# Odd head norms from PSUM, MLP squares behind the second ReLU, and masks made earlier in the solve

## The chip, the cores and the metric

The kernel runs on one core of a Trainium2 chip. The metric is the time of the program on the device in microseconds (us), as the median of several runs. The engines are TensorE (PE), VectorE (DVE), ScalarE (ACT) and GpSimd (POOL); SyncE (SP) only issues transfers. They run side by side and are ordered by semaphores.

## The reference, cut to what matters

A token matrix `x` of 256 x 1024 passes through a first block (two kinds of attention, and a retrieval feed-forward over 16384 experts) and a second block of two layers. The change touches the second block alone:

```
layer 0: proj = rms(h) @ w_in_e              # uv | qkv | z | beta | a
         a_out = gmlp(gelu(uv));  b_out = gated_delta_rule(...)   # triangular solves in chunks of 64
         h = h + concat(a_out, b_out) @ w_out_e
layer 1: q, k, v = split(rms(h) @ w_qkv_o)
         q = rms_heads(q, q_gain) * 64**-0.5;  k = rms_heads(k, k_gain)   # 16 pieces of 64 a row
         h = h + diff_attention(q, k, v) @ w_out_o
both:    h = h + square(relu(rms(h) @ w_mlp1)) @ w_mlp2          # 1024 -> 4096 -> 1024
         h = h + (p @ w_ple) * sigmoid(rms(h) @ w_gate)
```

## The kernel before

All matrices stay in SBUF as 128 partitions by two halves of the tokens (`t` = 0, 1: "block 0" and "block 1" of a result). The weights are streamed in 128x1024 chunks through a ring of four slots. SyncE loads `w_raw`; ScalarE rounds it to `w_hi` ("split", L1218); GpSimd makes the rest `w_lo` = `w_raw` - `w_hi` ("rest", L1705). TensorE then does three products for each pair of operands (high with high, high with low, low with high; L611 to L613 where the tokens are stationary, L647 to L649 where the weights are). The splits run three chunks ahead of TensorE. A slot is loaded again when both its `w_hi` and `w_lo` are made. Every engine has its program written out by hand; within an engine all is done in that order, and a wait holds up all that stands behind it. ScalarE's `split_to(j)` makes all splits below chunk j; GpSimd walks through the chunks j and does other things at marked places (`norm_at`, `FIRST[...] + 3`).

**The solve.** `SOLVE` is a list of 21 steps, numbered from 0, each with two halves of four 128x128 products (L1055) in a rotation of six PSUM banks. Results named in `PLAIN` are copied out by ScalarE (L1560), the others are added, subtracted or multiplied by VectorE (L2432 to L2449). Steps 6 and 7 are N4 and N4T (plain), 8 and 9 additions to YI and YIT, 10 is N8 (plain), 11 and 12 additions to YI and YIT, 13 is P1 (plain, from L1T and Y), 14 and 15 subtract from Y and YT, 16 is P2 (from L2T). L1T and L2T are `aT` times a mask. gmlp's mix (L1032) is put before step 11 on TensorE, and its product into OC (L2409) before step 12 on VectorE; TensorE transposes OC before step 15.

**The odd layer.** Groups q1, k1 and v1 have eight chunks each and leave four PSUM banks `acc`; the next group's first product into a bank waits until the bank is read. VectorE copies the banks with the row's factor (L1953), squares (L2557), sums (L2558), waits for ScalarE's root (L1631) and scales by the root and by the gain (L2563, L2564). TensorE transposes Q and K after v1.

**The MLP.** In each layer 64 chunks alternate: one of w_mlp1 whose result (`col`) is 128 hidden units for all tokens, and one of w_mlp2 that adds into `acc`. ScalarE takes ReLU and square (L1584, L1586), VectorE cuts the square into `H_hi` (L2503) and `H_lo` (L2505), and TensorE needs `H_lo` for the chunk of w_mlp2. Three chunks stand ahead of a loop of 15 rounds, one behind it. The row norm of the MLP isn't applied to its input but to its sum: ScalarE squares X (`row_squares`, L1234), GpSimd makes `rstd` (L1759 to L1761) and its square `rsq` (L1844), and VectorE uses `rsq` in the residual (L1964).

Of the kernel before, what the change touches and what calls it, by code (L numbers as in the profile page):

```python
# [33 lines left out]
ACT = mybir.ActivationFunctionType  # L34
# [3 lines left out]
P = 128  # L38
# [149 lines left out]
def share(semaphore, signals):  # L188


    base, shared = 0, {}
    for name, count in signals:
        shared[name] = (semaphore, base)
        base += count
    return shared
# [5 lines left out]
        "qk", "vc", "qup", "kvup", "br_a", "br_b", "wout", "v", "out_e", "mlp0", "ple0", "q1", "k1",  # L201
        "v1", "out_o", "mlp1", "ple1")]),
    **share("acc_read_act", [("ev_ga", 4), ("ev_gb", 4), ("ev_zba", 2), ("ev_uv", 4), ("ev_gate0", 4),
                             ("ev_gate1", 4)]),
# [28 lines left out]
def program(nc, ins, out):  # L233
    ctx = ExitStack()
    with ctx:
# [173 lines left out]
        L1T = big("L1T", 105, [P, NT, G_H, P])  # L409
        P1 = big("P1", 109, [P, NT, G_H, P])  # L410
        L2T = big("L2T", 113, [P, NT, G_H, P])
# [69 lines left out]
        ba = stat[:, 0:16].rearrange("p (t n) -> p t n", t=NT)  # L481
        sp_x, sp_d, sp_r = stat[:, 40:48], sq32[:, 0:8], sq32[:, 16:24]
# [718 lines left out]
        def _(act):  # L1201
# [371 lines left out]

            def mlp(layer):

                j0 = FIRST[f"mlp{layer}"]
                f0 = layer * D_FF // P

                def relu2(blk, j, i, s):
                    used(act, j, i)  # L1580
                    if layer or not (isinstance(blk, int) and blk < 2):

                        act.wait_ge(sem("H"), blk - 1 + f0)
                    f(H_r[:, s, :], col[s][:, 0:SEQ], ACT.Relu).then_inc(sem("relu"), 1)  # L1584
                    act.wait_ge(sem("relu"), blk + 1 + f0)
                    f(H_q[:, s, :], H_r[:, s, :], ACT.Square).then_inc(sem("square"), 1)  # L1586

                split_to(j0 + 4)
                relu2(0, j0, 0, 0)
                split_to(j0 + 5)  # L1590
                relu2(1, j0 + 1, 0, 1)
                split_to(j0 + MLP_SKIP + AHEAD)
                j = j0 + MLP_SKIP
                with act.Fori(0, MLP_ROUNDS) as r:
                    for q in range(4):
                        split(j + q + AHEAD, r)
                        if q % 2 == 0:
                            relu2(2 * r + 2 + q // 2, j + q, r, (q // 2) % 2)
                done[0] = j + 4 * MLP_ROUNDS + AHEAD
# [9 lines left out]
            def per_layer_in(layer):  # L1609

                nc.scalar.dma_start(p_raw[:, :, :], ins["p"][layer]).then_inc(sem("p_in"), 16)

# [3 lines left out]
            row_squares("ev_out_e", (1,))  # L1616
            per_layer_in(0)
# [6 lines left out]
            row_squares("x_ple0", (1,))  # L1624
            for m, nxt in enumerate(("k1", "v1")):
                split_to(FIRST[nxt] + 7)
                if m == 0:
                    act.wait_ge(sem("lam_dots"), upto("lam_dots", 2))
                    f(stat[:, 2:4], stat[:, 0:2], ACT.Exp).then_inc(sem("lam_exp"), 1)
                act.wait_ge(sem("qk_ss"), m + 1)  # L1630
                f(sq32[:, :], sq32[:, :], ACT.Sqrt, bias=epsc[:, 0:1], scale=1.0 / C_DH).then_inc(  # L1631
                    sem("qk_root"), 1)
# [31 lines left out]
            row_squares("ev_out_o", (1,))  # L1664
            per_layer_in(1)
# [6 lines left out]
        def _(pool):  # L1672
# [121 lines left out]
            def delta_and_gmlp_maps():  # L1794
# [14 lines left out]
                for t in range(NT):  # L1809
                    for m in range(M_G):  # L1810
# [14 lines left out]
            norm_at = [FIRST[name] + 3 for name in ("qk", "query", "zba", "mlp0", "ple0", "q1", "mlp1",  # L1825
                                                    "ple1")]
            j = 1
            while j < len(PLAN):
# [11 lines left out]
                for layer in range(2):  # L1840
                    if j == FIRST[f"mlp{layer}"] + 3:

                        have_rstd(pool, R_MLP[layer])
                        g.tensor_tensor(rsq, rstd[:, :], rstd[:, :], ALU.mult).then_inc(  # L1844
                            sem("rsq"), 1)
# [39 lines left out]
        def _(dve):  # L1885
# [515 lines left out]
            for s, (result, _, _, _) in enumerate(SOLVE):  # L2401
                if s == MIX_AT + 1:
# [24 lines left out]
                for t in range(NT):  # L2427
# [11 lines left out]
                    else:  # L2439
                        y = YIT if result.startswith("YT") else YI  # L2440
                        if s in (11, 12):

                            then(v.tensor_tensor(four(L1T if s == 11 else L2T, t), four(aT, t),
                                                 over(masks[:, 4 if s == 11 else 5, :], [P, 4, P], 1),
                                                 ALU.mult))
# [107 lines left out]
            for m, (g, src, gain) in enumerate((("q1", Q1, R_QG), ("k1", K1, R_KG))):  # L2553
                evac(g, half(src), R_ODD)
                x = src[:, :, :].rearrange("p t (n d) -> p (t n) d", d=C_DH)
                y = SQ[:, :, :].rearrange("p t (n d) -> p (t n) d", d=C_DH)
                then(v.tensor_tensor(y, x, x, ALU.mult))  # L2557
                then(v.tensor_reduce(sq32[:, :], y, AX_X, ALU.add), "qk_ss")  # L2558
                dve.wait_ge(sem("qk_root"), upto("qk_root", m + 1))
                then(v.reciprocal(sq32[:, :], sq32[:, :]))  # L2560
                if m == 0:
                    then(v.tensor_scalar(sq32[:, :], sq32[:, :], C_DH ** -0.5, None, ALU.mult))
                then(v.tensor_tensor(x, x, over(sq32[:, :], [P, 32, C_DH], 2), ALU.mult))  # L2563
                then(v.tensor_tensor(x, x, over(rows[:, gain:gain + C_DH], [P, 32, C_DH], 1),  # L2564
                                     ALU.mult), "qk1")
# [130 lines left out]
```

## Time and the profile before

| what | us |
|---|---|
| median of 3 runs | 1833.08 |
| lowest and highest run | 1833.07, 1841.83 |
| the profiled execution's own time | 1837.99 |
| its span, first to last instruction | 1836.3 |
| its mean granted TensorE clock | 0.98 |

All rows shown below are of the one profiled execution, with times from the start of its span. The profiled execution is 4.9 us above the median. The odd layer, the two MLPs and the solve lie behind 1140 us of the span.

### The profile page before, as it was taken

How to read it: one execution, taken by the hardware profiler on the slowest of the kernel's cores; microseconds unless marked ns; L12 is line 12 of the kernel's file. 1: busy time of each engine (PE TensorE's matmuls, PEld its weight loads, DVE VectorE, ACT ScalarE, POOL GpSimd, SP SyncE). 2: the span in 40 equal slices, each digit the busy share in tenths (PEclk: the TensorE clock that was granted, in tenths of full speed). 3: DMA queues.
4: the chain of work that ended last, by engine and by line, in shares of the span. 5: the costliest groups of instructions: out<-in, count | busy, mean ns of one | idle time of the engine just before them, and what ended most of it. 6: DMA issues, size and time to landing. Idle time of an engine off the chain costs nothing.

```text
span 1836.3 us, 32192 instructions
## 1 busy us (share of the span) xinstructions
PE 1746.2 (95%) x10852; PEld 1563.1 (85%) x10852; DVE 941.9 (51%) x1874; ACT 922.2 (50%) x1592; POOL 1051.6 (57%) x542
## 2 busy tenths in 40 slices
PE   8989899999999999999999999889999898799998
PEld 6767799999999998888888787878999776689996
DVE  6563229991777775555555657533111377431113
ACT  5555456666333334444555557325445644455454
POOL 7835578888666664000000087337888696478885
PEclk9999899999999999999999999999999998899999
DMA  6623365555444445555555554015555453145553
GB/s 199 178 81 115 115 218 163 182 182 185 148 138 140 142 144 173 194 193 192 191 192 193 195 172 134 23 60 163 185 184 189 153 163 124 47 156 191 185 188 109
DMA packets 81027, 288.23 MB, mean 157 GB/s; under 512 B 9264, under 2 KB 9264, under 8 KB 80432
## 3 DMA queue, kind: packets, MB, share of 16 engines
q1 hardware_dynamic: 80512, 286.10, 48.0%
q8 instruction: 50, 0.82, 0.2%
q10 hardware_dynamic: 432, 1.05, 0.1%
q14 instruction: 33, 0.27, 0.0%
HBM read 285.01 MB, written 2.10 MB: 156 GB/s over the span
## 4 chain that ended last, share of the span: by engine, by line
PE 86%; DVE 6%; ACT 4%; POOL 2%; issue 2%; DMA 0%; DVEq 0%; ACTq 0%; POOLq 0%
PE acc L611 14%; PE acc L612 14%; PE acc L613 14%; PE col L647 11%; PE col L648 11%; PE col L649 11%; PE mb L904 3%; POOL w_lo L1705 2%; PE acc L1055 1%; ACT hT_hi L1242 1%; PE mb L684 1%; ACT w_hi L1218 1%; PE col L1055 1%; PE mb L743 0%; PE mb L885 0%
## 5 line engine op out<-in xcount | busy, mean ns | idle before, releaser
L1705 POOL TENSOR_TENSOR w_lo<-w_raw,w_hi 128x1024 fp32r<-128x1024 f32 (+1 forms) x410 | 989.5, 2434 | 357.4 <-ACT w_hi L1218 357.1
L1218 ACT ACTIVATE w_hi<-w_raw 128x1024 fp32r<-128x1024 f32 (+1 forms) x539 | 565.8, 1053 | 397.7 <-PE acc L613 353.2
L647 PE MATMUL col<-hT_hi,w_hi 128*128 128x256 f32 x1632 | 467.8, 287 | 2.6 <-DVE hT_lo L1921 1.8
L649 PE MATMUL col<-hT_hi,w_lo 128*128 128x256 f32 x1632 | 461.6, 283 | 0.0
L648 PE MATMUL col<-hT_lo,w_hi 128*128 128x256 f32 x1632 | 461.5, 283 | 0.0
L647 PEld LDWEIGHTS col<-hT_hi,w_hi 128*128 128x128 f32 x1632 | 312.6, 192 | 5.8 <-issue 2.2
L648 PEld LDWEIGHTS col<-hT_lo,w_hi 128*128 128x128 f32 x1632 | 312.8, 192 | 2.4
L649 PEld LDWEIGHTS col<-hT_hi,w_lo 128*128 128x128 f32 x1632 | 312.4, 191 | 0.0
L611 PE MATMUL acc<-w_hi,W_hi 128*128 128x512 f32 x512 | 199.2, 389 | 0.0
L612 PE MATMUL acc<-w_lo,W_hi 128*128 128x512 f32 x512 | 199.2, 389 | 0.0
L613 PE MATMUL acc<-w_hi,W_lo 128*128 128x512 f32 x512 | 199.2, 389 | 0.0
L611 PE MATMUL acc<-w_hi,hT_hi 128*128 128x512 f32 (+2 forms) x432 | 170.6, 395 | 16.1 <-POOL w_lo L1705 6.0
L1747 POOL TENSOR_SCALAR_AFFINE_SELECT WST<-WST 128x512 f32<-128x512 f32 x1 | 0.6, 636 | 318.7 <-DMA WST<-in_gmlp_w 318.7
L2503 DVE CAST H_hi<-H_q 128x256 fp32r<-128x256 f32 x64 | 29.9, 467 | 292.4 <-ACT H_q L1586 292.4
L612 PE MATMUL acc<-w_lo,hT_hi 128*128 128x512 f32 (+2 forms) x432 | 168.1, 389 | 0.0
L613 PE MATMUL acc<-w_hi,hT_lo 128*128 128x512 f32 (+2 forms) x432 | 167.1, 388 | 0.0
L2264 DVE TENSOR_TENSOR w_lo<-w_raw,w_hi 128x1024 fp32r<-128x1024 f32 x128 | 156.8, 1225 | 2.0 <-ACT w_hi L1218 1.9
L2242 DVE TENSOR_TENSOR W_lo<-act_e,W_hi 128x256 fp32r<-128x256 f32 x128 | 54.5, 426 | 145.4 <-ACT W_hi L1427 144.8
L611 PEld LDWEIGHTS acc<-w_hi,hT_hi 128*128 128x128 f32 x432 | 82.7, 191 | 37.5 <-issue 15.3
L613 PEld LDWEIGHTS acc<-w_hi,W_lo 128*128 128x128 f32 x512 | 96.1, 188 | 20.1
L611 PEld LDWEIGHTS acc<-w_hi,W_hi 128*128 128x128 f32 x512 | 96.1, 188 | 20.0
L612 PEld LDWEIGHTS acc<-w_lo,W_hi 128*128 128x128 f32 x512 | 96.1, 188 | 19.8
(515 smaller groups left out, 2687.2 us busy)
## 6 DMA issues: line engine op xcount, KB each, us to landing
w_raw<-in_expert_u SPq DMA_DIRECT2D x128, 512.0 KB, 3.5
w_raw<-in_expert_v SPq DMA_DIRECT2D x128, 512.0 KB, 3.5
w_raw<-in_w_mlp SPq DMA_DIRECT2D x128, 512.0 KB, 3.4
w_raw<-in_w_in SPq DMA_DIRECT2D x24, 512.0 KB, 3.7
w_raw<-in_w_qkv_o SPq DMA_DIRECT2D x24, 512.0 KB, 3.6
w_raw<-in_w_query SPq DMA_DIRECT2D x16, 512.0 KB, 3.5
w_raw<-in_w_gate SPq DMA_DIRECT2D x16, 512.0 KB, 3.4
w_raw<-in_w_qkv_e SPq DMA_DIRECT2D x12, 512.0 KB, 4.1
```

Source lines behind the costliest of these rows:

```text
L611: mm(o, hi(t), w_hi[:, s, a:b], start=first, stop=False)
L612: mm(o, hi(t), w_lo[:, s, a:b], start=False, stop=False)
L613: m = mm(o, lo(t), w_hi[:, s, a:b], start=False, stop=last)
L647: mm(o, wh[:, k, :], hi[:, k, :], start=k == 0, stop=False)
L648: mm(o, wh[:, k, :], lo[:, k, :], start=False, stop=False)
L649: m = mm(o, wl[:, k, :], hi[:, k, :], start=False, stop=k == KD - 1)
L904: m = mm(mb[s % 2][:, t * P:(t + 1) * P], hot2[:, s % 2, t, :], hot1[:, s % 2, t, :], start=True, stop=True)
L1055: m = mm(solve_banks[n % 6][:, h * P:(h + 1) * P], maps[lhsT][:, t, h, :], maps[rhs][:, t, h, :], start=True, stop=True)
L1218: f(w_hi[:, s, 0:w], w_raw[:, s, 0:w], ACT.Copy).then_inc(sem(f"hi{s}"), 1)
L1705: g.tensor_tensor(w_lo[:, s, 0:w], w_raw[:, s, 0:w], w_hi[:, s, 0:w].bitcast(F32), ALU.subtract).then_inc(sem(f"lo{s}"), 1)
L2242: v.tensor_tensor(lo[:, q, :], act_e[:, c, :], hi[:, q, :].bitcast(F32), ALU.subtract).then_inc(sem("W_lo"), 1)
L2264: v.tensor_tensor(w_lo[:, s, :], w_raw[:, s, :], w_hi[:, s, :].bitcast(F32), ALU.subtract).then_inc(sem(f"lo{s}"), 1)
```

## The change

Three places are edited.

1. **Solve.** The four mask products for L1T and L2T are taken out of steps 11 and 12 and made at steps 6 and 7, in other places of SBUF (57 and 97, where N1T and N1 have been read for the last time). gmlp's product moves from before step 12 to before step 13.
2. **Odd layer.** The squares for the head norms move from VectorE (from Q or K in SBUF) to ScalarE, which reads the PSUM bank after VectorE has copied it; the bank is free for TensorE when ScalarE is through. The factors `head_r` and the gains `head_gain` lie in PSUM banks `col[0]` and `col[1]`, so that the two scalings take one operand from SBUF and one from PSUM.
3. **MLP.** ScalarE's squares of block 1 for the MLP's norm stand behind the second ReLU rather than ahead of the first; so does p's transfer, ahead of the second ReLU. GpSimd takes the MLP's norm and `rsq` at the first chunk of ple rather than at the fourth chunk of the MLP.

```diff
-        "qk", "vc", "qup", "kvup", "br_a", "br_b", "wout", "v", "out_e", "mlp0", "ple0", "q1", "k1",
+        "qk", "vc", "qup", "kvup", "br_a", "br_b", "wout", "v", "out_e", "mlp0", "ple0",
+    **share("raw_qk1", [("raw_q1", 4), ("raw_k1", 4)]),
-                             ("ev_gate1", 4)]),
+                             ("ev_q1", 4), ("ev_k1", 4), ("ev_gate1", 4)]),
-        L1T = big("L1T", 105, [P, NT, G_H, P])
+        L1T = big("L1T", 57, [P, NT, G_H, P])
-        L2T = big("L2T", 113, [P, NT, G_H, P])
+        L2T = big("L2T", 97, [P, NT, G_H, P])
+        head_r = col[0][:, 0:32]
+        head_gain = col[1][:, 0:2 * C_DH]
...
                 split_to(j0 + 5)
+                per_layer_in(layer)
                 relu2(1, j0 + 1, 0, 1)
+                row_squares("ev_out_o" if layer else "ev_out_e", (1,))
                 split_to(j0 + MLP_SKIP + AHEAD)
...
             row_squares("ev_out_e", (0,))
             turned(T_MLP[0])
-            row_squares("ev_out_e", (1,))
-            per_layer_in(0)
             mlp(0)
...
+            def head_squares(g):
+
+                for t in range(NT):
+                    for n in range(2):
+                        act.wait_ge(sem("raw_" + g), upto("raw_" + g, 2 * t + n + 1))
+                        f(SQ[:, t, n * 512:(n + 1) * 512], acc[2 * t + n][:, :], ACT.Square,
+                          scale=rstd[:, t:t + 1]).then_inc(sem("ev_" + g), 1)
             for m, nxt in enumerate(("k1", "v1")):
+                split_to(FIRST[nxt] + 3)
+                have_rstd(act, R_ODD)
+                if m == 1:
+
+                    act.wait_ge(sem("qk_ss"), 1)
+                head_squares(("q1", "k1")[m])
                 split_to(FIRST[nxt] + 7)
...
-            norm_at = [FIRST[name] + 3 for name in ("qk", "query", "zba", "mlp0", "ple0", "q1", "mlp1",
-                                                    "ple1")]
+            norm_at = [FIRST[name] + 3 for name in ("qk", "query", "zba", "ple0", "q1", "ple1")]
...
-                    if j == FIRST[f"mlp{layer}"] + 3:
-
+                    if j == FIRST[f"ple{layer}"]:
+
+                        row_rstd()
                         have_rstd(pool, R_MLP[layer])
...
             for s, (result, _, _, _) in enumerate(SOLVE):
-                if s == MIX_AT + 1:
+                if s in (6, 7):
+                    for t in range(NT):
+                        then(v.tensor_tensor(four((L1T, L2T)[s - 6], t), four(aT, t),
+                                             over(masks[:, s - 2, :], [P, 4, P], 1), ALU.mult))
+                if s == MIX_AT + 2:
...
-                        if s in (11, 12):
-
-                            then(v.tensor_tensor(four(L1T if s == 11 else L2T, t), four(aT, t),
-                                                 over(masks[:, 4 if s == 11 else 5, :], [P, 4, P], 1),
-                                                 ALU.mult))
...
-            for m, (g, src, gain) in enumerate((("q1", Q1, R_QG), ("k1", K1, R_KG))):
-                evac(g, half(src), R_ODD)
+            assert R_KG == R_QG + C_DH
+            dve.wait_ge(sem("hT"), KD * (T_ODD + 1))
+            then(v.tensor_copy(head_gain, rows[:, R_QG:R_QG + 2 * C_DH]))
+            have_rstd(dve, R_ODD)
+            for m, (g, src) in enumerate((("q1", Q1), ("k1", K1))):
+                for t, n, a in banks(g):
+                    go(v.tensor_scalar(half(src)(t, n), a[:, :], rstd[:, t:t + 1], None, ALU.mult),
+                       "raw_" + g)
                 x = src[:, :, :].rearrange("p t (n d) -> p (t n) d", d=C_DH)
                 y = SQ[:, :, :].rearrange("p t (n d) -> p (t n) d", d=C_DH)
-                then(v.tensor_tensor(y, x, x, ALU.mult))
+                dve.wait_ge(sem("ev_" + g), upto("ev_" + g, 4))
                 then(v.tensor_reduce(sq32[:, :], y, AX_X, ALU.add), "qk_ss")
                 dve.wait_ge(sem("qk_root"), upto("qk_root", m + 1))
-                then(v.reciprocal(sq32[:, :], sq32[:, :]))
+                then(v.reciprocal(head_r, sq32[:, :]))
                 if m == 0:
-                    then(v.tensor_scalar(sq32[:, :], sq32[:, :], C_DH ** -0.5, None, ALU.mult))
-                then(v.tensor_tensor(x, x, over(sq32[:, :], [P, 32, C_DH], 2), ALU.mult))
-                then(v.tensor_tensor(x, x, over(rows[:, gain:gain + C_DH], [P, 32, C_DH], 1),
-                                     ALU.mult), "qk1")
+                    then(v.tensor_scalar(head_r, head_r, C_DH ** -0.5, None, ALU.mult))
+                dve.wait_ge(sem("raw_" + g), upto("raw_" + g, 4))
+                then(v.tensor_tensor(x, x, over(head_r, [P, 32, C_DH], 2), ALU.mult))
+                then(v.tensor_tensor(x, x, over(head_gain[:, m * C_DH:(m + 1) * C_DH],
+                                                [P, 32, C_DH], 1), ALU.mult), "qk1")
```

The same two lines are taken out ahead of `mlp(1)`.

## Rows read from the trace of the kernel before

**Rows 1.** The page: busy us (share of the span) and instructions of each engine.

```profile
PE 1746.2 (95%) x10852; PEld 1563.1 (85%) x10852; DVE 941.9 (51%) x1874; ACT 922.2 (50%) x1592; POOL 1051.6 (57%) x542
```

**Rows 2.** Waits of TensorE, 1140 to 1836: engine line waited for, us, times, longest.

```profile
PE acc L611 <- DVE H_lo L2505: 6.5, 2, 3.2
...
PE acc L1055 <- DVE YIT L2447: 3.9, 1, 3.9
...
PE acc L611 <- DVE K L1953: 2.5, 1, 2.5
PE acc L611 <- POOL w_lo L1705: 2.4, 2, 1.4
```

**Rows 3.** Timeline, TensorE in the solve: start, us, instruction, [idle before <-releaser].

```profile
1165.06 1.95 PE L1032 MATMUL mb<-UV,WST 128*128 128x128 f32 x16
...
1176.95 2.07 PE L1055 MATMUL acc<-P,YIT 128*128 128x128 f32 x8 [3.94 <-DVE YIT L2447]
...
1188.32 1.13 PE L1055 MATMUL col<-VBt,YIT 128*128 128x128 f32 x8
```

**Rows 4.** Timeline, VectorE, GpSimd and ScalarE in the solve.

```profile
1160.86 0.69 DVE L2447 TENSOR_TENSOR YI<-acc,YI 128x512 f32<-128x512 f32 x1 [3.78 <-PE acc L1055]
...
1168.01 1.62 DVE L2443 TENSOR_TENSOR L1T<-aT,masks 128x512 f32<-128x512 f32 x1 [3.77 <-PE acc L1055]
...
1171.84 2.16 DVE L2409 SCALAR_TENSOR_TENSOR OC<-mb,cols,UV 128x128 f32<-128x128 f32 x8
...
1176.21 0.69 DVE L2447 TENSOR_TENSOR YIT<-acc,YIT 128x512 f32<-128x512 f32 x1
...
1158.57 3.45 POOL L1813 TENSOR_SCALAR UV<-UV,gsum,gvar 128x128 f32<-128x128 f32 x8
1162.10 2.36 POOL L1816 TENSOR_TENSOR UV<-UV,rows 128x1024 f32<-128x1024 f32 x1
...
1171.60 0.60 ACT L1560 ACTIVATE P<-acc 128x512 f32<-128x512 f32 x1 [5.75 <-PE acc L1055]
```

**Rows 5.** Busy time by stretches: us, busy of each engine, PEclk, DMA share, GB/s.

```profile
1176.90:1183.40 6.50, 6.45 (x32) 6.45 (x33) 1.38 (x2) 1.20 (x2) 0.00 (x0) 0.53 0.00 0
...
1251.60:1254.60 3.00, 2.94 (x7) 2.37 (x8) 2.97 (x4) 0.00 (x0) 2.23 (x1) 0.50 0.74 239
```

**Rows 6.** Timeline, VectorE, GpSimd and ScalarE: the odd layer; first row the solve's start.

```profile
1126.12 1.22 DVE L2367 TENSOR_TENSOR Kt<-Kt,col 128x1024 f32<-128x1024 f32 x1
...
1485.78 2.73 DVE L1953 TENSOR_SCALAR Q<-acc,rstd 128x512 f32<-128x512 f32 x4 [4.53 <-PE acc L613]
...
1502.15 4.42 DVE L2563 TENSOR_TENSOR Q<-Q,sq 128x2048 f32<-128x2048 f32 x1
...
1470.98 71.84 POOL L1705 TENSOR_TENSOR w_lo<-w_raw,w_hi 128x1024 fp32r<-128x1024 f32 x25
...
1490.50 1.06 ACT L1218 ACTIVATE w_hi<-w_raw 128x1024 fp32r<-128x1024 f32 x1 [1.66 <-PE acc L613]
```

**Rows 7.** Timeline, ScalarE, GpSimd and VectorE at the start of the first MLP.

```profile
1243.65 0.68 ACT L1234 ACTIVATE junk<-X 128x512 f32<-128x512 f32 x1
...
1244.88 1.10 ACT L1218 ACTIVATE w_hi<-w_raw 128x1024 fp32r<-128x1024 f32 x1
...
1246.58 7.26 POOL L1705 TENSOR_TENSOR w_lo<-w_raw,w_hi 128x1024 fp32r<-128x1024 f32 x3
...
1246.73 2.39 DVE L2503 CAST H_hi<-H_q 128x256 fp32r<-128x256 f32 x1 [1.85 <-ACT H_q L1586]
1249.16 2.45 DVE L2505 TENSOR_TENSOR H_lo<-H_q,H_hi 128x256 fp32r<-128x256 f32 x1
...
1260.23 0.42 DVE L2505 TENSOR_TENSOR H_lo<-H_q,H_hi 128x256 fp32r<-128x256 f32 x1
```

**Rows 8.** Timeline, GpSimd and VectorE at the end of the first MLP.

```profile
1418.25 4.76 POOL L1705 TENSOR_TENSOR w_lo<-w_raw,w_hi 128x1024 fp32r<-128x1024 f32 x2 [0.86 <-ACT w_hi L1218]
...
1423.20 0.42 DVE L2505 TENSOR_TENSOR H_lo<-H_q,H_hi 128x256 fp32r<-128x256 f32 x1
```

More of the change, by code:

```diff
@@ L1572, in _, with per_layer_in @@
             split_to(FIRST["out_e"] + KD)
+            def per_layer_in(layer):
+                nc.scalar.dma_start(p_raw[:, :, :], ins["p"][layer]).then_inc(sem("p_in"), 16)
             def mlp(layer):
@@ L1607, in gated_projection @@
                          f"ev_gate{layer}", R_PLE[layer])
-            def per_layer_in(layer):
-                nc.scalar.dma_start(p_raw[:, :, :], ins["p"][layer]).then_inc(sem("p_in"), 16)
             split_to(FIRST["mlp0"] + 3)
@@ L1663, in _ @@
             turned(T_MLP[1])
-            row_squares("ev_out_o", (1,))
-            per_layer_in(1)
             mlp(1)
```

## The prediction

> **What bounds the kernel now.** The page comes first: TensorE is busy for 95% of the span, every other engine for 57% or less [rows 1]. So an edit pays only where it removes idle or slow time of TensorE. The view of TensorE's waits, from 1140 us on, then says which of its stops this change can touch: two for `H_lo` (6.5 us together), one for `YIT` (3.9), one for `K` (2.5) and two for `w_lo` (2.4) [rows 2]. That is 15.3 us. The timelines around each stop say who was late and why, and the table by stretches says what the stop costs behind itself: 1176.9 to 1183.4 ran at a granted clock of 0.53 and 1251.6 to 1254.6 at 0.50 [rows 5], near the 1.2 GHz level, right behind a stop. All changed parts lie before a common end, and TensorE streams weights between them, so time saved at one is not given back at the next unless something else is late.
>
> **The solve.** Step 12's `YT+` of block 1 starts at 1176.21 and takes 0.69 us; TensorE then starts the first product with P1 at 1176.95, after 3.94 us of idling [rows 3, 4]. In front of that `YT+` on VectorE lie four mask products (1.62, the first, and three of 0.69, as the `YIT` row) and gmlp's product (2.16) [rows 4]. Now the four are made at steps 6 and 7. They need 4 x 0.72 = 2.9 us; the `YI` row of step 8 shows VectorE idle for 3.78 us in front of it, until 1160.86 [rows 4]. So they are hidden on VectorE itself. Without them and the product, step 11 takes its two PSUM results as they come, from 1168.0, and the four additions of steps 11 and 12 go back to back at about 0.9 us, TensorE's pace for eight products: they end at about 1171.4 instead of 1176.9. ScalarE's copy of P1, 1171.60 to 1172.20, is now last; with 0.15 us for the signal TensorE starts at 1172.35 instead of 1176.95: 4.6 us saved. gmlp's product runs 1171.4 to 1173.6, under the two `Y-` products of TensorE; the first subtraction could otherwise start at about 1173.5, so it costs 0.1. The transposes of OC wait for the product and come behind those two, at about 1174.1, so they don't wait. If this cover were gone, the price would be the whole 2.16.
>
> Behind the stop the slow clock goes too, if the stop does. 6.5 us at 0.53 are 6.5 x 0.47 = 3.1 us lost; stepping through the chain (products at 0.9, additions 0.7, copies 0.6) I get the start of u at 1180.8, against 1188.32 [rows 3]: 7.5 us in all, of which 2.9 are clock.
>
> The mask products read two SBUF tensors, and GpSimd works on UV from 1158.57 for 3.45 us and on the gains from 1162.10 for 2.36, which gmlp's mix on TensorE needs at 1165.06 [rows 3, 4]. The first mask product took 1.62 instead of 0.69 beside GpSimd, so the two disturb each other. Two of the four now fall behind 1158.5. At best they cost GpSimd nothing; at worst it is late by 2 x 0.69 = 1.4, less the 0.6 between the end of the gains (1164.46) and the mix, so 0.8 us. I take the worse end, since the trace shows such pairs giving way to each other. Solve: 7.5 - 0.8 = **6.7 saved** (bounds: 3.7 if the slow clock comes anyway, to 7.5).
>
> **The odd head norms.** The squares leave VectorE, and the two scalings of Q and of K take one operand from PSUM. `Q<-Q,sq` took 4.42 us while GpSimd ran 25 `w_lo` back to back in 71.84 us, 2.87 each, where its plain one takes 2.40 [rows 6]. A product of 128x1024 with one operand in PSUM took 1.22 at a time when GpSimd was busy, so 2.4 for 2048. So VectorE is through with Q after about 1505.5 rather than 1511.0 and K's banks are copied as they fill (0.68 each): the 2.5 us stop at v1 goes. GpSimd keeps some 0.3 us a chunk on TensorE's 2.72 (ScalarE's split and its wait for TensorE, 1.06 + 1.66 [rows 6]), and the 2.4 us for `w_lo` go. Added: each bank is freed only after VectorE's copy and then ScalarE's square (0.60, as the copy of P1, from PSUM). Both go at TensorE's pace of 0.68 a bank, so this is one delay: copy from 1485.78 to 1486.5, square to 1487.2, and TensorE wants the bank at 1487.4. The margin is 0.2 us; I set 0.1 for each of the two groups. ScalarE's splits behind the squares are 1.3 us later, against three chunks (8 us) of lead. The new copy of the gains (128x128) lies in VectorE's idle time. Odd part: 4.9 - 0.2 = **4.7 saved** (bounds 0 to 5.2). The Trainium skill ("PSUM — Partial Sum Buffer", "PSUM bank collisions raise a hardware error") forbids two engines on one bank at once, reads included, so copy and square can't overlap; that is the series that I priced, and no run here shows the collision itself.
>
> **The MLP starts.** ScalarE's two squares of block 1 start at 1243.65 and delay the split behind them to 1244.88; GpSimd waits for those squares, takes the norm, and only then makes three `w_lo` in a row (7.26 us from 1246.58). VectorE's cast `H_hi` (2.39) and `H_lo` (2.45) stand beside them, each ending just after a `w_lo` ends; in the loop the same `H_lo` takes 0.42 [rows 7]. This is the 3.2 us stop. In the new order:
> - split of chunk 3 from 1243.7, its `w_lo` 1244.9 to 1247.3;
> - the first ReLU can't start before its product's end, which gains it only 0.2 us: the square is ready at 1246.5 (the cast stood at 1246.73);
> - cast `H_hi` waits for the `w_lo`: 1247.4; `H_lo` 1247.43 to 1247.86;
> - the next `w_lo` starts when ScalarE's next split is ready, 1247.6, so behind `H_lo`;
> - TensorE ends its second product at 1248.3 and goes on without a stop.
>
> That is 2 x 3.25 = 6.5 saved, and the low clock behind each (3.0 us at 0.50 [rows 5], the second alike: 1.5 each) 3.0 more, so **9.5** (bounds 2.8 to 9.9). Moved: the two squares (1.23 us) now stand ahead of the split of chunk 5, which then is ready on GpSimd at 1254.0 and wanted at 1256.6; GpSimd is late by one pair and VectorE's third block gets through at about 1259.0, wanted at 1259.5; a round later GpSimd has its 0.8 us of idling back. p's transfer is issued some 5 us later, lands by 1250 and is wanted by the end of the MLP only; VectorE waits for it with nothing due before 1255. GpSimd's norm (two powers of 0.6, four small steps of some 0.25, the factor and the signals between: about 2.6 us) now stands ahead of `w_lo` of ple's first chunk: from 1420.6, half way through the pair of 1418.25, to 1423.2 [rows 8]. That chunk is then ready at about 1425.6 and wanted at 1427.2; the factor for the residual is ready before 1425. But `H_lo` of the last block starts at 1423.20, a tie with that `w_lo`. I take it that VectorE's cast just before holds GpSimd's last small step back, and set nothing; if lost, the last product starts 1.3 late.
>
> **The sum.** 6.7 + 4.7 + 9.5 = 20.9 us. The profiled execution took 1837.99 (span 1836.3), so 1817.1. The median of the runs is 4.9 lower, 1833.08; I carry the same difference: 1833.1 - 20.9 = **1812.2**.
>
> **The rivals.**
> (a) *The stall only moves.* At the MLP start everything hangs on `H_lo` starting 0.17 us before a `w_lo`. If GpSimd is first, `H_lo` ends at about 1250.2, TensorE starts at 1250.25 instead of 1251.66, and idles 2 us, with the slow clock still behind it. Each MLP gives 1.4, both 2.8 instead of 9.5: 1833.1 - 14.2 = 1818.9. The Trainium skill ("SBUF — State Buffer", "Who interferes with whom") says this: the shared pair goes to whoever issues first, for the whole instruction. The trace agrees with 2.39 and 2.45 against 0.42 [rows 7]. Chance 0.17.
> (b) *The tie at the MLP's end is lost.* 2 x 1.3 back: 1814.8. Chance 0.10.
> (c) *The odd part does not do what it says*: the scalings stay at 4.4 us with GpSimd late, and the squares come on top of the bank's way. v1 then starts 0.6 later than now and the 4.7 are gone: 1833.1 - 20.9 + 4.7 + 0.6 = 1817.5. Against it is the 1.22 us row [rows 6]. Chance 0.08.
> (d) *The clock in the solve falls anyway*, for reasons other than the 3.94 us stop: 1815.1. Chance 0.07.
> (e) *Slower.* In the MLP loops GpSimd, set back by the squares, never regains its idle time, and every round's `H_lo` waits for a `w_lo`. With 15 rounds in each of two MLPs the 20.9 us are used up from 0.70 us a round on; at 1 us a round the time is 1833.1 + 9.1 = 1842.2. Against it: GpSimd has 4.76 us of work and 0.86 of idling in a round [rows 8]. Chance 0.03.
> The forecast itself has 0.52, small other things 0.03.
>
> **Range and chances.** The forecast's own range is 1808 (GpSimd not disturbed in the solve, another slow stretch gone) to 1816. (a), (c) and (d) reach 1819, so 1807 to 1819.5 leaves out (e) and the tails. A difference of 0.5% is 9.2 us, about what tells a change of this kernel from none. Faster by more needs 1823.9 or less: all but (e) and two mishaps together, so 0.92; within 0.05; slower 0.03.
>
> **What would show it.** Right: no stop for `YIT` near 1172; u's products start some 6.5 us earlier; Q's and K's scalings at 2.3 us each; GpSimd not solid through the odd group; `H_lo` of block 0 at 0.4 us, and the granted clock at 1.0 behind it. Wrong: an `H_lo` over 1 us at either end of an MLP, a wait of gmlp's mix for UV over 0.9 us, or a stop of k1 or v1 for ScalarE's squares.

## The result, and the profile after

The changed kernel takes 1825.22 us (median of 8 runs, 1821.46 to 1830.18), the kernel before 1840.32 us in 8 runs beside it (1833.07 to 1847.25). The ratio is **0.9927, 95% interval 0.9903 to 0.9951**: faster, by 0.7%. The prediction said 1812.2 us and 0.9886 of the kernel before. So the sign is right, but the time lies above the range of 1807 to 1819.5, and the gain is two thirds of the forecast.

The profiled execution went from a span of 1836.3 us to 1822.7 us. The page's line of busy time hardly moves:

```profile
PE 1744.2 (96%) x10852; PEld 1561.4 (86%) x10852; DVE 922.4 (51%) x1873; ACT 927.5 (51%) x1600; POOL 1041.5 (57%) x542
```

Read against [rows 1]: VectorE lost 19.5 us of work, ScalarE took 5.3 over, GpSimd lost 10.1. None of them is the bound, so this says nothing yet about the gain. What TensorE waited for, in the stretch of [rows 2] (engine line waited for: us, times, longest), says more:

```profile
PE mb L746 <- DVE PR L2634: 6.4, 6, 3.3
PE acc L614 <- DVE H_lo L2519: 6.0, 4, 1.7
PE mb L687 <- DVE hT_lo L1950: 5.6, 1, 5.6
```

The stops for `YIT`, `K` and `w_lo` are gone. Those for `H_lo` are not: 6.5 us in two became 6.0 us in four.

To see where each microsecond went, cut both traces at the first matmul of each stage. TensorE's busy time by such stretches, of the kernel after (stretch, us, busy, granted clock as PEclk, share of DMA, GB/s):

```profile
1140.59:1179.39 38.80, 36.52 (x313) 1.00 0.13 42
1179.39:1231.71 52.32, 46.83 (x257) 0.90 0.18 52
1231.71:1422.42 190.71, 186.83 (x1181) 0.99 0.56 180
1453.02:1597.88 144.86, 128.63 (x585) 0.89 0.37 113
1597.88:1786.99 189.11, 185.24 (x1182) 1.00 0.57 181
```

They are the solve, the rest of the mixer, the first MLP with the start of its gated projection, the odd layer, and the second MLP likewise. The same cuts before, after, and in the experiments below (us; "ahead" is all before the solve, where no edit of any kernel here lies):

| kernel | ahead | solve | rest of mixer | MLP 0 | odd layer | MLP 1 |
|---|---|---|---|---|---|---|
| before | 1142.45 | 45.87 | 51.16 | 190.44 | 149.39 | 190.68 |
| after | 1140.59 | 38.80 | 52.32 | 190.71 | 144.86 | 189.11 |
| solve_only | 1142.10 | 38.77 | 51.15 | 190.58 | 149.41 | 190.67 |
| odd_only | 1140.68 | 45.94 | 51.18 | 190.46 | 142.98 | 190.67 |
| mlp_only | 1143.76 | 44.36 | 49.59 | 189.17 | 149.53 | 190.69 |
| both_ends | 1143.94 | 38.78 | 51.17 | 189.08 | 144.11 | 190.67 |
| h_psum | 1146.47 | 38.79 | 52.30 | 185.57 | 143.50 | 185.57 |
| before_h_psum | 1141.87 | 45.89 | 51.18 | 185.59 | 149.83 | 185.58 |
| norm_late | 1146.43 | 38.73 | 52.41 | 189.16 | 143.36 | 187.58 |
| squares_only | 1146.13 | 45.83 | 55.82 | 189.08 | 146.02 | 190.69 |
| psum_only | 1143.15 | 45.98 | 51.13 | 190.51 | 142.91 | 190.67 |
| masks_only | 1144.09 | 39.86 | 50.74 | 191.65 | 149.81 | 191.65 |
| product_only | 1142.14 | 41.19 | 52.74 | 190.40 | 149.39 | 190.67 |
| h_psum_old_order | 1146.44 | 38.76 | 52.42 | 185.57 | 143.57 | 185.58 |

The 13.6 us between the two spans are 1.9 ahead of every edit (chance), 7.1 in the solve, -1.2 in the mixer behind it, -0.3 in the first MLP, 4.5 in the odd layer and 1.6 in the second MLP. So the solve and the odd layer gave about what was forecast, and the MLP term, 9.5 us, is where the time is missing: 1.3 us came. Each figure is from one profile of each kernel.

**The start of the first MLP, after.** ScalarE, GpSimd, VectorE and TensorE (start, us; in brackets the idle time before and its releaser), to hold against [rows 7]:

```profile
1238.23 0.42 ACT L1593 ACTIVATE H_q<-H_r 128x256 f32<-128x256 f32 x1
...
1238.55 1.04 ACT L1221 ACTIVATE w_hi<-w_raw 128x1024 fp32r<-128x1024 f32 x1
...
1237.13 4.91 POOL L1720 TENSOR_TENSOR w_lo<-w_raw,w_hi 128x1024 fp32r<-128x1024 f32 x2 [4.35 <-ACT w_hi L1221]
...
1238.68 1.00 DVE L2517 CAST H_hi<-H_q 128x256 fp32r<-128x256 f32 x1 [1.58 <-ACT H_q L1593]
1239.72 2.60 DVE L2519 TENSOR_TENSOR H_lo<-H_q,H_hi 128x256 fp32r<-128x256 f32 x1
...
1242.37 0.52 PE L614 MATMUL acc<-w_hi,H_hi 128*128 128x512 f32 x1 [1.73 <-DVE H_lo L2519]
```

The cast waited out GpSimd's first `w_lo` (1.00 us, until 1239.68). But ScalarE's split had ended at 1239.59. GpSimd started the second `w_lo` of the pair at 1239.67, and `H_lo`, at 1239.72, came 0.05 us behind it. `H_lo` took 2.60 us, until that `w_lo` was through. TensorE idled 1.73 us. Behind the stop the granted clock was at 0.50, in the second of these stretches (us, busy of PE, PEld, DVE, ACT, POOL, PEclk, DMA share, GB/s):

```profile
1240.00:1243.00 3.00, 1.27 (x8) 1.03 (x7) 2.96 (x4) 2.28 (x7) 2.04 (x1) 0.95 0.64 236
1243.00:1246.00 3.00, 3.00 (x8) 2.35 (x8) 1.01 (x2) 0.69 (x1) 2.24 (x1) 0.50 0.54 175
```

**The end of the first MLP, after**, GpSimd, VectorE, TensorE, against [rows 8]:

```profile
1413.92 0.23 POOL L1859 TENSOR_TENSOR sum<-rstd 128x2 f32<-128x2 f32 x1
1414.12 7.28 POOL L1720 TENSOR_TENSOR w_lo<-w_raw,w_hi 128x1024 fp32r<-128x1024 f32 x3
...
1413.81 0.29 DVE L2517 CAST H_hi<-H_q 128x256 fp32r<-128x256 f32 x1 [4.86 <-ACT H_q L1593]
1414.14 2.65 DVE L2519 TENSOR_TENSOR H_lo<-H_q,H_hi 128x256 fp32r<-128x256 f32 x1
...
1416.84 0.50 PE L614 MATMUL acc<-w_hi,H_hi 128*128 128x512 f32 x1 [1.27 <-DVE H_lo L2519]
```

GpSimd's `w_lo` started at 1414.12, `H_lo` 0.02 us behind it: the tie that the prediction named is lost, and TensorE stops 1.27 us where it did not stop before.

### The profile page after: what moved, and what is told of

It reads as the page before. It is cut to its first block, busy times and chain, and to the rows that moved or that the text cites. A ratio compares the mean times of both kernels' runs of the same rounds, so it can differ in the third digit from the quotient of the medians.

```text
span 1822.7 us, 32204 instructions
## 1 busy us (share of the span) xinstructions
PE 1744.2 (96%) x10852; PEld 1561.4 (86%) x10852; DVE 922.4 (51%) x1873; ACT 927.5 (51%) x1600; POOL 1041.5 (57%) x542
## 4 chain that ended last, share of the span: by engine, by line
PE 87%; DVE 5%; ACT 3%; POOL 3%; issue 2%; DMA 0%; DVEq 0%; ACTq 0%; POOLq 0%
PE acc L614 14%; PE acc L615 14%; PE acc L616 14%; PE col L650 11%; PE col L651 11%; PE col L652 11%; PE mb L907 3%; POOL w_lo L1720 2%; PE acc L1058 1%; PE mb L687 1%; DVE H_lo L2519 1%; ACT hT_hi L1245 1%; ACT w_hi L1221 0%; PE mb L746 0%; DVE hT_lo L1936 0%
## 5 line engine op out<-in xcount | busy, mean ns | idle before, releaser
L1720 POOL TENSOR_TENSOR w_lo<-w_raw,w_hi 128x1024 fp32r<-128x1024 f32 (+1 forms) x410 | 977.7, 2403 | 359.4 <-ACT w_hi L1221 358.8
L2517 DVE CAST H_hi<-H_q 128x256 fp32r<-128x256 f32 x64 | 22.7, 355 | 294.8 <-ACT H_q L1593 294.8
```

The costliest lines, as they stand in the source:

```text
L1720: g.tensor_tensor(w_lo[:, s, 0:w], w_raw[:, s, 0:w], w_hi[:, s, 0:w].bitcast(F32), ALU.subtract).then_inc(sem(f"lo{s}"), 1)
L2517: v.tensor_copy(H_hi[:, s, :], H_q[:, s, :]).then_inc(sem("H_hi"), 1)
```

## The experiments

All were timed in five rounds beside the kernel before. Diffs are against the kernel before unless said otherwise.

**The three parts alone.** solve_only, odd_only and mlp_only hold the hunks of one part each: the masks and gmlp's product; `head_squares`, `head_r` and `head_gain`; the second half of the squares, p's transfer and GpSimd's norm.

> Only the solve's edit. Theory 1 (the three parts are independent, each worth what its stretch shows between the traces of before and after): the stretch from the solve's start to the transposes ahead of the first MLP is 5.9 us shorter, no stop for YIT, all behind it as before; time 0.32% below before (0.9968). Theory 2 (the parts only work together, or the clock evens them out): the whole-kernel gain is under 2 us, since the low clock falls elsewhere instead.

> Only the odd layer's edit. Theory 1: the stretch from the odd layer's transposes to those ahead of the second MLP is 4.5 us shorter; no stop of v1 for K, none for w_lo; time 0.25% below before (0.9975). Theory 2: under 2 us in the whole.

> Only the MLP's edit. Theory 1 (the stop at the MLP's start is only shortened, because GpSimd's second w_lo starts some 0.1 us ahead of VectorE's H_lo, and a second tie is lost at the end): four stops for H_lo of 1.3 to 1.7 us, both MLP stretches together 1.3 us shorter than before, time within 0.1% of before. Rival (the edit is good, and what ate it is that the solve came first and shifted the clock): about 9 us below before (0.995).

Measured: solve_only **0.9961** (0.9943 to 0.9978), odd_only **0.9959** (0.9944 to 0.9975), mlp_only **0.9986** (0.9970 to 1.0002). In the table solve_only is 7.1 us shorter in the solve and odd_only 6.4 us in the odd layer, and neither differs in any other stretch by over 0.4 (but for odd_only's 1.8 ahead of every edit). Both are more than was expected of them, 5.9 and 4.5, which were the changed kernel's own figures. mlp_only has the same four stops for `H_lo` as the changed kernel, and gains 1.3 and 0.0 us in its MLPs; its time can't be told from the kernel before. So the MLP part misses its 9.5 us on its own, without the other two. In the changed kernel some 3 us of what the parts give alone are not there as well, in the mixer behind the solve and in the odd layer.

**Both ends put in order by waits** (both_ends), against the changed kernel:

```diff
                 for layer in range(2):
+                    if j == FIRST[f"mlp{layer}"] + 3:
+                        pool.wait_ge(sem("H"), layer * D_FF // P + 1)
-                    if j == FIRST[f"ple{layer}"]:
+                    if j == FIRST[f"ple{layer}"] + 1:
```

> The changed kernel, with two edits to GpSimd alone: it waits for the first H_lo of each MLP before it makes w_lo of chunk 3, and it takes the MLP's norm behind w_lo of ple's first chunk instead of ahead of it. Theory 1 (the shared access of VectorE and GpSimd, and who is first, is all that is behind the stops): all four stops for H_lo go, and the low clock behind the two at the starts; 2 x 1.7 + 2 x 1.5 + 2 x 1.3 = 9 us below the changed kernel, so about 0.9878 of before. Rival (GpSimd is simply too busy there): the stops come back two or three chunks later as waits for w_lo or for H_lo, and the time is that of the changed kernel (0.9927) or worse.

Measured: **0.9954** (0.9936 to 0.9972), no better than the changed kernel and by the midpoints worse: the rival held. The stops at the ends are gone and those at the starts have moved. (The profiled execution took 1825.78 us, the shortest of its six, whose median is 1831.04. So the table shows this kernel at its best, and what makes its median worse than the changed kernel's stays open.) VectorE and TensorE at the first MLP's start:

```profile
1244.51 2.52 DVE L2521 TENSOR_TENSOR H_lo<-H_q,H_hi 128x256 fp32r<-128x256 f32 x1
1246.95 2.62 DVE L1923 CAST p_hi<-p_raw 128x512 fp32r<-128x512 f32 x1
1249.61 2.77 DVE L1924 TENSOR_TENSOR p_lo<-p_raw,p_hi 128x512 fp32r<-128x512 f32 x1
1252.69 2.08 DVE L2519 CAST H_hi<-H_q 128x256 fp32r<-128x256 f32 x1 [0.32 <-DVE p_lo L1924]
1254.81 2.45 DVE L2521 TENSOR_TENSOR H_lo<-H_q,H_hi 128x256 fp32r<-128x256 f32 x1
...
1257.32 0.50 PE L614 MATMUL acc<-w_hi,H_hi 128*128 128x512 f32 x1 [3.25 <-DVE H_lo L2521]
```

Held back once, GpSimd has seven `w_lo` to make without a pause (17.59 us from 1241.92). Each instruction of VectorE gets its turn only between two of them, so the five in these rows take 12.4 us, where `H_lo` alone takes 0.42 in the loop [rows 7]. TensorE's stop, now 3.25 us, comes back two blocks later. Winning one tie is no cure.

**The shared resource taken away** (h_psum on the changed kernel, before_h_psum on the kernel before). ScalarE writes its square `H_q` to two PSUM banks that the MLP leaves unused, so that `H_hi` reads no SBUF tensor and `H_lo` only one:

```diff
-        H_q = big("H_q", 39, [P, 2, SEQ])
+        H_q = [mb[i][:, 0:SEQ] for i in range(2)]
-                    f(H_q[:, s, :], H_r[:, s, :], ACT.Square).then_inc(sem("square"), 1)
+                    f(H_q[s], H_r[:, s, :], ACT.Square).then_inc(sem("square"), 1)
-                    v.tensor_copy(H_hi[:, s, :], H_q[:, s, :]).then_inc(sem("H_hi"), 1)
+                    v.tensor_copy(H_hi[:, s, :], H_q[s]).then_inc(sem("H_hi"), 1)
-                    v.tensor_tensor(H_lo[:, s, :], H_q[:, s, :], H_hi[:, s, :].bitcast(F32),
+                    v.tensor_tensor(H_lo[:, s, :], H_q[s], H_hi[:, s, :].bitcast(F32),
```

> The changed kernel, with one more edit: ScalarE writes the MLP's squares H_q to two PSUM banks (the mixer's mb[0] and mb[1], unused there), so VectorE's cast H_hi and its H_lo read at most one SBUF tensor. All else as in the changed kernel; nothing is left out. Theory (VectorE's two-operand SBUF work and GpSimd's w_lo exclude each other, and that alone makes the four H_lo stops of 1.7, 1.7, 1.3 and 1.3 us): all four go, H_lo takes about 0.45 us everywhere, and the low clock right behind the first MLP's start goes too; about 6 us of stops and up to 3 us of clock below the changed kernel, so near 0.988 of the kernel before. Rival 1 (GpSimd is simply late and the stop returns for w_lo or two blocks later, as when it was held back): waits of TensorE for w_lo or H_lo of 2 to 3 us stay, and the ratio stays at 0.993 to 0.996. Rival 2 (the port is not it, H_lo is long because of its own operands): H_lo still takes 2.4 to 2.6 us beside w_lo. Rival 3: squares from ScalarE to PSUM and reads of PSUM cost more in every block and the MLP loops get slower.

> The kernel before with the same single edit (H_q in two PSUM banks), the squares of the norm still ahead of the MLP's start. Theory: at each MLP's start GpSimd still makes three w_lo in a row, but H_hi and H_lo run beside them at 0.4 to 0.7 us instead of 2.4; both 3.2 us stops go, and the low clock behind them; 6.5 to 9.5 us below the kernel before, ratio about 0.995 to 0.996. Rival (the stop hangs on ScalarE being late, or on w_lo of chunk 3 coming late through the norm): a stop of over 1 us for w_lo or H_lo stays at the start, and the ratio is 0.998 or more.

Measured: h_psum **0.9895** (0.9878 to 0.9912; 1818.51 us beside 1838.56), before_h_psum **0.9952** (0.9932 to 0.9971). GpSimd and VectorE of h_psum at the first MLP's start:

```profile
1242.98 4.95 POOL L1720 TENSOR_TENSOR w_lo<-w_raw,w_hi 128x1024 fp32r<-128x1024 f32 x2 [4.35 <-ACT w_hi L1221]
...
1244.50 0.42 DVE L2517 CAST H_hi<-mb 128x256 fp32r<-128x256 f32 x1 [1.55 <-ACT mb L1593]
1244.96 0.42 DVE L2519 TENSOR_TENSOR H_lo<-mb,H_hi 128x256 fp32r<-128x256 f32 x1
```

The order of the work is that of the changed kernel and the pair of `w_lo` stands just as there. The cast `H_hi` starts 1.52 us into the first of the pair (1.55 in the changed kernel), but it is not held back, and both it and `H_lo` are through, in 0.42 us each, before that `w_lo` ends. All four stops are gone, and so is the low clock; both MLP stretches of h_psum:

```profile
1237.56:1423.13 185.57, 184.69 (x1181) 168.26 (x1180) 35.05 (x80) 97.05 (x150) 155.25 (x72) 1.00 0.57 183
1597.27:1782.84 185.57, 184.69 (x1182) 168.27 (x1180) 35.04 (x80) 97.07 (x150) 155.26 (x72) 1.00 0.56 183
```

and those of before_h_psum, in the old order of the work:

```profile
1238.94:1424.53 185.59, 184.71 (x1181) 168.27 (x1180) 38.22 (x80) 97.05 (x150) 157.28 (x76) 1.00 0.57 185
1604.98:1790.56 185.58, 184.69 (x1182) 168.27 (x1181) 38.25 (x80) 97.07 (x150) 157.35 (x76) 1.00 0.56 185
```

The first number behind each stretch is its length. One edit of four lines takes 4.9 and 5.1 us from the kernel before and 5.1 and 3.5 us from the changed kernel's.

GpSimd and VectorE of before_h_psum at the first MLP's start show that it is the operand and not the moment that counts, to hold against [rows 7]:

```profile
1246.03 10.12 POOL L1705 TENSOR_TENSOR w_lo<-w_raw,w_hi 128x1024 fp32r<-128x1024 f32 x4
...
1246.16 0.42 DVE L2503 CAST H_hi<-mb 128x256 fp32r<-128x256 f32 x1 [1.82 <-ACT mb L1586]
1246.62 0.43 DVE L2505 TENSOR_TENSOR H_lo<-mb,H_hi 128x256 fp32r<-128x256 f32 x1
...
1249.57 1.50 DVE L1906 CAST p_hi<-p_raw 128x512 fp32r<-128x512 f32 x1
1251.11 2.78 DVE L1907 TENSOR_TENSOR p_lo<-p_raw,p_hi 128x512 fp32r<-128x512 f32 x1
```

All four stand beside `w_lo` without a pause. The two that read PSUM take their usual time, where they took 2.39 and 2.45 us before. The two that read SBUF alone are held back still: in h_psum, where no `w_lo` runs beside them, `p_hi` and `p_lo` take 0.42 and 0.69 us.

The Trainium skill ("SBUF — State Buffer", "Who interferes with whom") says that an instruction of VectorE with at most one SBUF input, outside its two-port modes, does not contend with GpSimd, and that one with two contends with a GpSimd instruction that reads SBUF. For `H_lo` the traces agree: 0.42 and 0.43 us with one SBUF input, 2.60 and 2.45 with two. The cast `H_hi`, with one SBUF input, was held back as well (2.39 us in [rows 7]); whether it runs in such a mode no run here shows.

**The tie at the end alone** (norm_late): the changed kernel with GpSimd's norm steps one `w_lo` later, `FIRST[f"ple{layer}"] + 1`.

> The changed kernel with GpSimd's norm steps one w_lo later at each MLP's end (behind the w_lo of the gated projection's first chunk instead of ahead of it). Theory (the tie at the end is who is first; the norm steps hold that w_lo back to 1414.1, 0.03 us before H_lo): w_lo and H_lo swap, the two stops of 1.3 us at the MLP ends go or the w_lo now starts ahead and H_lo comes behind it earlier; up to 2.6 us below the changed kernel. Rival (GpSimd has too much work there anyway): the stops at the ends stay at 1 us or more and the time is that of the changed kernel. The two stops of 1.7 us at the starts stay in both.

Measured: **0.9923** (0.9904 to 0.9941), which by itself can't be told from the changed kernel. Its profile is clear: two stops for `H_lo` are left, of 1.7 us, and MLP 0 and MLP 1 are 1.55 and 1.53 us shorter than in the changed kernel. GpSimd and VectorE at the end of MLP 0:

```profile
1415.06 4.75 POOL L1720 TENSOR_TENSOR w_lo<-w_raw,w_hi 128x1024 fp32r<-128x1024 f32 x2 [0.86 <-ACT w_hi L1221]
...
1420.01 0.43 DVE L2519 TENSOR_TENSOR H_lo<-H_q,H_hi 128x256 fp32r<-128x256 f32 x1
```

So it is the place of the norm, ahead of that `w_lo`, that lost the tie.

**The order of the work, with the resource gone** (h_psum_old_order): the solve and odd parts and `H_q` in PSUM, with the MLP part undone.

> The changed kernel with H_q in PSUM, and with the MLP part of the change undone: the second half of the squares and GpSimd's norm are back ahead of the MLP. Theory (once VectorE and GpSimd no longer exclude each other there, the place of the squares and of the norm is worth nothing): each MLP's stretch is 185.6 us as with the new order, the ratio is that of the changed kernel with H_q in PSUM, 0.9895 within its interval. Rival (the new order is worth something of its own): 1 us or more per MLP slower, with a stop for w_lo or H_lo at the start, ratio 0.9905 or more.

Measured: **0.9890** (0.9867 to 0.9914), MLP stretches of 185.57 and 185.58 us. So the place of the squares, of p's transfer and of the norm is worth nothing that shows once `H_hi` and `H_lo` are not held back. This kernel and h_psum have the lowest ratios of all and can't be told apart.

**The two halves of the odd part.** squares_only has ScalarE's squares, with the factors and gains left in SBUF; psum_only has the factors and gains in PSUM, with the squares left on VectorE:

```diff
 squares_only:
+        head_r = sq32[:, :]
+        head_gain = rows[:, R_QG:R_QG + 2 * C_DH]
 psum_only:
+        head_r = col[0][:, 0:32]
+        head_gain = col[1][:, 0:2 * C_DH]
+            then(v.tensor_copy(head_gain, rows[:, R_QG:R_QG + 2 * C_DH]))
...
                 then(v.tensor_tensor(y, x, x, ALU.mult))
```

> The kernel before with one half of the odd part alone: ScalarE makes the head squares from the PSUM banks, but the factors of the heads and the gains stay in SBUF. Theory (the gain of the odd part is that VectorE's scalings no longer exclude GpSimd, plus the 4.4 us product gone): the scalings of Q and K stay at 4.4 us beside w_lo and GpSimd stays back to back through them; the K stop goes since the squares (4.4 us each) are off VectorE, but stops for w_lo stay or shrink partly; 2 to 5 us below the kernel before instead of 6.4. Rival (the squares on VectorE were the whole of it): the full 6.4 us of the odd stretch, no w_lo stop left.

> The kernel before with the other half of the odd part alone: the head factors and the gains lie in PSUM, the squares stay on VectorE. Theory (VectorE's scalings and GpSimd's w_lo exclude each other only while both operands are in SBUF): the two scalings of Q and of K take about 2.3 us each instead of 4.4 for some of them; GpSimd regains idle time and the stop for w_lo shrinks, but the squares (4.4 us each) still hold VectorE and GpSimd, so the stop for K shrinks by at most what the scalings gave. By the odd stretch's 149.4 us before, 143.0 with the whole part and 146.0 with the squares moved alone, the two halves sum if they are independent: 146.0 here, ratio about 0.998. Rival (each half alone removes the same stop): 144.5 or less. Rival (neither works without the other): 148.5 or more.

Measured: squares_only **0.9988** (0.9972 to 1.0005), which can't be told from the kernel before, with the odd layer 3.4 us shorter (its mixer, untouched, was 4.7 us longer in the profile, at a granted clock of 0.85); psum_only **0.9971** (0.9951 to 0.9992), 6.5 us shorter, which is all that the whole part gives (6.4). The halves don't add up; my theory there fell, and its rival held: the PSUM half alone removes the stop for `K` and both for `w_lo`. (The stretch says this better than single stops do: product_only below, with the odd layer untouched, shows no stop for `K` either, but 2.8 us for `w_lo` and the same 149.4 us in all.) In psum_only VectorE's squares still take 4.18 and 3.38 us and GpSimd still makes its 25 `w_lo` without a pause, but in another time than in [rows 6]:

```profile
1489.42 4.18 DVE L2561 TENSOR_TENSOR SQ<-Q 128x2048 f32<-128x2048 f32 x1
...
1501.75 2.29 DVE L2567 TENSOR_TENSOR Q<-Q,col 128x2048 f32<-128x2048 f32 x1
1504.08 2.29 DVE L2568 TENSOR_TENSOR Q<-Q,col 128x2048 f32<-128x2048 f32 x1
...
1471.85 63.82 POOL L1707 TENSOR_TENSOR w_lo<-w_raw,w_hi 128x1024 fp32r<-128x1024 f32 x25
```

That is 2.55 us each instead of 2.87, and below TensorE's 2.72 a chunk. In squares_only one product of `Q` takes 4.38 us and stops for `w_lo` of 1.8 us in all are left.

**The two halves of the solve part.** masks_only makes `L1T` and `L2T` at steps 6 and 7, product_only changes `MIX_AT + 1` to `MIX_AT + 2`.

> The kernel before with L1T and L2T made at steps 6 and 7, gmlp's product left ahead of step 12. Theory (VectorE's load between steps 11 and 12 is the stop): the stop for YIT at step 13 shrinks from 3.9 us by what two to four masks took, but the product's 2.16 us still stand ahead of step 12, so 1.5 to 2 us of it stay; the low clock may stay too; the solve's stretch, 45.9 us before and 38.8 with both, comes to 41 to 44. Rival (the masks alone are the cause): 39 to 40 us, and no stop over 0.5.

> The kernel before with gmlp's product made one step later (ahead of step 13), L1T and L2T left where they were. Theory: the stop for YIT shrinks by about 2 us to 1.5 to 2; the solve's stretch comes to 41 to 44 us; with masks_only it adds up to the 7.1 us of both only if the low clock goes with either. Rival (the clock falls only once the stop is long enough): one of the two shows the granted clock at about 0.5 behind the stop and the other does not.

Measured: masks_only **0.9991** (0.9976 to 1.0006), product_only **0.9990** (0.9972 to 1.0009). In the profiles the stop for `YIT` is 0.92 and 1.74 us, and the solve 6.0 and 4.7 us shorter: added, more than the 7.1 of both, since with either half alone the low clock behind the stop is gone. product_only came as its theory said; masks_only's stop and solve are shorter than its theory had them (1.5 to 2 us, 41 to 44), and the stop is longer than its rival's 0.5. The stretch behind that stop, of masks_only and then of product_only, to hold against the 0.53 of [rows 5]:

```profile
1175.40:1181.90 6.50, 6.48 (x57) 6.44 (x58) 3.69 (x6) 1.68 (x3) 0.00 (x0) 1.00 0.00 0
```

```profile
1174.50:1181.00 6.50, 6.36 (x55) 6.17 (x56) 5.48 (x14) 1.61 (x3) 0.00 (x0) 1.00 0.00 0
```

Neither time can be told from the kernel before, and both ratios are smaller gains than these stretches; in masks_only both MLPs are 1.0 to 1.2 us longer with the same stops, product_only's mixer 1.6 us. Why the medians keep so little of 6.0 and 4.7 us stays open: one profile doesn't tell where the low clock falls in the other runs.

## Why the prediction was right and wrong

**The solve: right.** Forecast 6.7 us, measured 7.1. The four masks took 1.42 + 1.49 us, hidden; the product 2.16, its cover held; P's copy and `YIT` were in time and TensorE shows no stop; the clock stayed at 1.00. UV was late as feared, but by less: its steps took 4.38 us instead of the 3.45 of [rows 4], so it was 0.9 late and not 1.4, and gmlp's mix waited 0.22 us for it instead of 0.8. In the changed kernel 1.2 us came back in the rest of the mixer, by a granted clock of 0.90 where it was 0.93; solve_only and both_ends, with the same solve, don't show that, and the others with it do (52.3 to 52.4); what decides it stays open.

**The odd layer: right in its stops, in part by luck in its time.** Forecast 4.7 us, measured 4.5 in the changed kernel and 6.4 alone, which is over the upper bound of 5.2. TensorE's idle time in the stretch fell by 5.4 and 5.1 us, near the 4.9 of the stops; the rest is its busy time for the same work, 0.9 us longer in the changed kernel at a granted clock of 0.89, and 1.3 shorter in odd_only at 0.92, where it was 0.91. The scalings are at 2.29 us, the stops for `K` and `w_lo` are gone, and the bank's longer way, copy then square, costs nothing that shows. But I let the moved squares carry part of the gain; psum_only shows that they carry none. Rival (c) did not happen.

**The MLPs: the step that failed.** It is "the next `w_lo` starts when ScalarE's next split is ready, 1247.6, so behind `H_lo`". The forecast gave `H_lo` a lead of 0.17 us on that `w_lo`; the trace gives it a lag of 0.05, at 1239.72 against 1239.67. It had the split end 1.1 us and the cast 0.9 us behind the square; they ended 0.94 and 1.03 us behind it. Two errors of some 0.15 us turned the sign, and with it most of the 9.5 us went. `H_lo` took 2.60 us at the start and 2.65 at the end, which is the first of the signs of being wrong that the prediction names. With it rival (a) came true: a stop of 1.73 us (2 forecast) with the low clock still behind it. And so did rival (b), "I take it that VectorE's cast just before holds GpSimd's last small step back, and set nothing": the cast (0.29 us) held nothing back, and the `w_lo` went first by 0.02 us. The two were priced in the prediction one at a time, with 0.17 and 0.10; together they give the MLP part 2.8 - 2.6 = 0.2 us, and the time 1821.5 that follows is already outside the range. Measured were 1.3 us, and that too hangs on luck: in the changed kernel MLP 0 has the low clock behind its start and is 0.3 us longer than before, MLP 1 has not and is 1.6 shorter; in mlp_only MLP 1 is as before and MLP 0, at a mean clock of 1.00, is 1.3 shorter. before_h_psum shows that the 9.5 was a good figure for what the stops and the clock are worth (4.9 + 5.1 = 10.0 us from the kernel before); what the reordering got of it is 1.3.

**The base: a second step that failed.** "The median of the runs is 4.9 lower, 1833.08; I carry the same difference" rests on three runs, the first of the eight, and two of them are the shortest of all eight. The eight have 1840.3, and three more series of 22 to 29 runs 1838.6 to 1840.9. Of the 13.0 us between 1812.2 and 1825.2, 7.2 are this and 5.8 the smaller gain. Either error alone would have left the time inside: with 1840.3 as a base the range would have ended at 1826.7, and with the full gain the changed kernel would have been at some 1819.4. From profile to profile, where the base plays no part, 13.6 us came of 20.9: 8.2 are missing in the MLPs, 1.2 in the mixer and 0.2 in the odd layer, and 0.4 more in the solve and 1.9 by chance ahead of it stand against them.

## What to carry to other kernels

When two engines exclude each other for the length of an instruction, and a short instruction's start lies within some tenths of a microsecond of a long one's, do not forecast the winner's time alone: take both outcomes with about even chances, and price the ties of one kernel together. Look first for an operand that can live elsewhere: moving `H_q` to PSUM took 10 us off the two MLPs, and holding back or reordering the same work got 1 to 4 of them. And before an absolute time is forecast with a narrow range, run the kernel before often enough that its median is known more closely than that range.

## What the runs showed of the hardware

- A stop's length alone doesn't decide whether the clock falls behind it. In one and the same profile, that of the changed kernel, both MLPs start with a stop of 1.73 us for `H_lo`. Behind the first the granted clock was 0.50, near the 1.2 GHz level, for 3 us (above); behind the second it stayed at 1.00:

```profile
1608.50:1611.50 3.00, 2.96 (x13) 1.00 0.66 212
```

  That is most of why MLP 0 is 1.6 us longer there than MLP 1. The prediction took the fall for granted behind every such stop; what decides it no run here shows.
- Code that no edit touches varies with it: the part ahead of the solve took 1140.6 to 1146.5 us in the 14 profiles, and the mixer behind the solve 49.6 to 55.8, at a granted clock of 0.85 in the longest (squares_only) and 0.93 in the kernel before. A stage's gain is to be read from its own stretch, and one of under some 2 us from several profiles.
- GpSimd pays little in these ties, and VectorE pays nearly all: three `w_lo` in a row, the first beside a blocked `H_lo`, took 7.28 us (2.43 each, 2.40 alone), while `H_lo` took 2.65 instead of 0.42. Where VectorE's instructions are longer, GpSimd pays too: 2.87 us a `w_lo` in [rows 6] beside products of 128x2048 with both inputs in SBUF, 2.55 with the scalings' second input in PSUM, and in the solve 4.38 instead of 3.45 us for its eight small steps on UV beside two mask products of 128x512.
- From PSUM the cast `H_hi` takes 0.42 us (0.29 from SBUF) and `H_lo` 0.42 either way; ScalarE's square takes 0.39 into PSUM and 0.42 into SBUF.
